# Half of a depthwise convolution's taps on GpSimd, and ten fp32 weight pieces split in two

## The reference

```python
proj = h @ w_in[l]
q, k, v, qi, ki, wi, u, ga, gb = jnp.split(proj, split_at, axis=-1)
y_attn = dsa_attention(q, k, v, qi, ki, wi) @ w_attn_proj[l]     # top 64 keys of a row, softmax over them
y_conv = conformer_conv(u, w_dw[l], b_dw[l], conv_ln_g[l], conv_ln_b[l]) @ w_conv_proj[l]
merged = jax.nn.sigmoid(ga) * y_attn + jax.nn.sigmoid(gb) * y_conv

def conformer_conv(u, w_dw, b_dw, ln_g, ln_b):
    a, g = jnp.split(u, 2, axis=-1)
    z = a * jax.nn.sigmoid(g)
    z = lax.conv_general_dilated(z, w_dw, window_strides=(1,), padding=[(CONV_WIDTH - 1, 0)],
                                 feature_group_count=CONV_CH, ...) + b_dw
    return jax.nn.silu(layernorm(z, ln_g, ln_b))
```

## Time and profile before

| | |
|---|---|
| median of three runs | 954.34 us (953.24 to 954.71) |
| span of the profiled execution, first to last instruction | 953.0 us |
| PE busy | 918.4 us (96%) |
| VectorE busy | 627.9 us (66%) |
| ScalarE busy | 458.5 us (48%) |
| GpSimd busy | 31.7 us (3%), 42 instructions |
| taps on VectorE, L1914 | 120 of 489 ns on average |
| residues on VectorE, L1696 | 267 of 1223 ns |
| native matmuls, L597 | 80 records of 604 ns |
| granted TensorE clock | 0.996 of full speed |

### The profile page before, as it was taken

The page is one execution under the profiler, slowest core; times in us unless marked ns, Lnnn a source line. Parts: engine busy times, 40 slices in busy tenths (PEclk is TensorE's granted clock), DMA queues, the critical chain, the costliest instruction groups (busy, mean ns, idle before and its releaser), DMA issues.

```text
span 953.0 us, 11982 instructions
## 1 busy us (share of the span) xinstructions
PE 918.4 (96%) x4235; PEld 735.6 (77%) x4235; DVE 627.9 (66%) x1022; ACT 458.5 (48%) x709; POOL 31.7 (3%) x42
## 2 busy tenths in 40 slices
PE   4999999999999999999999999999999999999997
PEld 3877755688788888887887777788888788888785
DVE  4898999988755555676748445678656565555444
ACT  0554523465544444443654554674545465555442
POOL 2110000010000000000000000000000000000000
PEclk9999999999999999999999999999999999999999
DMA  9999324656485565575555343455451475655531
GB/s 331 353 386 352 114 79 145 232 204 219 134 265 180 190 192 187 195 263 171 189 190 184 91 152 112 133 177 199 149 204 46 133 221 183 190 193 182 177 133 44
DMA packets 103030, 178.10 MB, mean 187 GB/s; under 512 B 6318, under 2 KB 52635, under 8 KB 102986
## 3 DMA queue, kind: packets, MB, share of 16 engines
q1 hardware_dynamic: 96138, 151.23, 48.2%
q0 software_dynamic: 6848, 26.28, 7.5%
HBM read 176.39 MB, written 1.05 MB: 186 GB/s over the span
## 4 chain that ended last, share of the span: by engine, by line
PE 74%; DVE 12%; issue 7%; DMA 3%; ACT 2%; SPq 0%; POOL 0%; DVEq 0%; POOLq 0%; ACTq 0%
PE bank L564 18%; PE bank L566 18%; PE bank L565 18%; PE bank L976 10%; DVE conv_out L1914 5%; DVE w_lo L1696 2%; DMA tap_rows<-in_w_dw 1%; DMA raw_weights<-in_w_in 1%; ACT w_hi L1232 1%; PE bank L955 1%; DVE ada_acc L1772 1%; PE bank L643 1%; DMA ada_raw<-in_w_ada 1%; PE bank L795 1%; PE bank L635 1%
## 5 line engine op out<-in xcount | busy, mean ns | idle before, releaser
L1696 DVE TENSOR_TENSOR w_lo<-raw_weights,w_hi 128x1024 fp32r<-128x1024 f32 x267 | 324.2, 1223 | 229.2 <-ACT w_hi L1232 227.8
L1232 ACT ACTIVATE w_hi<-raw_weights 128x1024 fp32r<-128x1024 f32 x267 | 281.0, 1059 | 282.1 <-PE bank L566 200.3
L564 PE MATMUL bank<-w_hi,a_hi 128*128 128x512 f32 x808 | 323.5, 400 | 3.1 <-issue 1.3
L566 PE MATMUL bank<-w_hi,a_lo 128*128 128x512 f32 x808 | 315.9, 391 | 0.0
L565 PE MATMUL bank<-w_lo,a_hi 128*128 128x512 f32 x808 | 315.6, 391 | 0.0
L564 PEld LDWEIGHTS bank<-w_hi,a_hi 128*128 128x128 f32 x808 | 152.1, 188 | 40.6 <-issue 8.5
L566 PEld LDWEIGHTS bank<-w_hi,a_lo 128*128 128x128 f32 x808 | 152.1, 188 | 32.7
L565 PEld LDWEIGHTS bank<-w_lo,a_hi 128*128 128x128 f32 x808 | 152.4, 189 | 29.7 <-issue 0.2
L976 PE MATMUL bank<-w_hi,ff_hi 128*128 128x512 f32 x176 | 55.1, 394 | 0.8 <-DVE hidden_rows L2194 0.5
L976 PE MATMUL bank<-w_lo,ff_hi 128*128 128x512 f32 x176 | 54.2, 389 | 0.0
L976 PE MATMUL bank<-w_hi,ff_lo 128*128 128x512 f32 x176 | 54.2, 389 | 0.0
(11 more groups left out here) (264 smaller groups left out, 860.2 us busy)
## 6 DMA issues: line engine op xcount, KB each, us to landing
raw_weights<-in_w_in SPq DMA_DIRECT2D x40, 1024.0 KB, 5.1
raw_weights<-in_w_ffn_in SPq DMA_DIRECT2D x44, 512.0 KB, 4.6
raw_weights<-in_w_gate_up SPq DMA_DIRECT2D x44, 512.0 KB, 4.6
ada_start<-in_w_ada POOLq DMA_DIRECT2D x11, 1024.0 KB, 10.8
raw_weights<-in_w_ffn_out SPq DMA_DIRECT2D x9, 1024.0 KB, 4.9
raw_weights<-in_w_down SPq DMA_DIRECT2D x9, 1024.0 KB, 4.9
ada_raw<-in_w_ada POOLq DMA_DIRECT2D x8, 1024.0 KB, 8.3
raw_weights<-in_w_out SPq DMA_DIRECT2D x8, 1024.0 KB, 5.1
```

The lines of the kernel that those rows point to most:

```text
L564: pe.matmul(ps, hi[:, kt, ts], wh, start=start, stop=False)
L566: return pe.matmul(ps, lo[:, kt, ts], wh, start=False, stop=stop)
L1232: act.activation(w_hi[:, slot, 0:m], raw[:, b % RAW, half * PIECE:half * PIECE + m], ACT.Copy)\
L1696: dve.tensor_tensor(w_lo[:, slot, 0:m], raw[:, b % RAW, half * PIECE:half * PIECE + m], w_hi[:, slot, 0:m], ALU.subtract).then_inc(lo_read ...
```

## The change

Three things go together.

1. **`CG_DVE = 2`.** VectorE does only the taps of groups 0 and 1, 62 in place of 124. `A1_TAPS` becomes 1, eight times 4, and 3, so that they end in step 9; the 26 taps beside the selection stay in number and place.
2. **GpSimd does groups 2 and 3**, in a new `conv_taps` between its blocks 17 and 18. It has no single instruction for multiply and add here, so a tap is a `tensor_scalar` into one of four slots of `tap_products` (128x256) and a `tensor_tensor` that adds the slot to `conv_out`; with two first taps that carry the bias that is 62 and 60 instructions. Each has its own wait: an addition for its product and for the addition before it to the same group, a product for the addition that last used its slot. `tap_products` lies in the memory of `final_g`, so the load of `norm_final_g` moves on SP's queue from among the weights to behind `conv_lo`. `ln_mean` on PE waits for both engines.
3. **`NATIVE_LAST = 24`** leaves no native piece: pieces 25 to 34 are rounded by ScalarE, have residues on VectorE and three products on PE. Block 17 needs no wait for them.

```diff
-NATIVE_FIRST, NATIVE_LAST = 25, 34
+NATIVE_FIRST, NATIVE_LAST = 25, 24
-A1_TAPS = (1,) + (9,) * 10 + (7,)
+A1_TAPS = (1,) + (4,) * 8 + (3,)
...
-    final_g = sb("final_gain_rows", [P, D])
+    final_at = region(D * 4)
+    final_g = sb("final_gain_rows", [P, D], at=final_at)
+    tap_products = sb("tap_products", [P, 4, SEQ], at=final_at)
...
-        sp.dma_start(final_g[:], a["norm_final_g"].partition_broadcast(P)).then_inc(final_landed, 16)
...
         sp.wait_ge(sem["conv_lo"], 2)
+        sp.dma_start(final_g[:], a["norm_final_g"].partition_broadcast(P)).then_inc(final_landed, 16)
         sp.dma_start(mem_rows[:], a["mem_2"].rearrange("o (t p) d -> p (o t) d", p=P)).then_inc(sem["mem_landed"], 16)
...
-            if n == 17:
-                pool.wait_ge(piece_used, NATIVE_LAST + 1)
...
-        for n in range(14, 20):
+        for n in range(14, 18):
+            ada_block(n)
+
+        def conv_taps():
+            pool.wait_ge(sem["pad_zeroed"], 1)
+            pool.wait_ge(sem["conv_in"], 2)
+            pool.wait_ge(sem["vec_copied"], 2)
+            half = CG - CG_DVE
+            total = half * TAPS
+            for g in range(CG_DVE, CG):
+                pool.tensor_scalar(conv_out[:, g, :], conv_in[:, g, 0:SEQ], taps[:, g, 0:1],
+                                   vt[:, V_BDW + g:V_BDW + g + 1], ALU.mult, ALU.add).then_inc(sem["conv_done_pool"], 1)
+            for m in range(half, total + 1):
+                if m < total:
+                    g, k = CG_DVE + m % half, m // half
+                    if m >= half + 4:
+                        pool.wait_ge(sem["conv_done_pool"], m - 3)
+                    pool.tensor_scalar(tap_products[:, m % 4, :], conv_in[:, g, k:k + SEQ], taps[:, g, k:k + 1], None,
+                                       ALU.mult).then_inc(sem["conv_product"], 1)
+                if m > half:
+                    q = m - 1
+                    g = CG_DVE + q % half
+                    pool.wait_ge(sem["conv_product"], q - half + 1)
+                    pool.wait_ge(sem["conv_done_pool"], q - half + 1)
+                    pool.tensor_tensor(conv_out[:, g, :], conv_out[:, g, :], tap_products[:, q % 4, :], ALU.add)                        .then_inc(sem["conv_done_pool"], 1)
+
+        conv_taps()
+        for n in range(18, 20):
             ada_block(n)
...
-            pe.wait_ge(sem["conv_done"], CG * TAPS)
+            pe.wait_ge(sem["conv_done"], CG_DVE * TAPS)
+            pe.wait_ge(sem["conv_done_pool"], (CG - CG_DVE) * TAPS)
...
-            for m in range(taps_done[0], min(taps_done[0] + n, CG * TAPS)):
-                g, k = m % CG, m // CG
+            for m in range(taps_done[0], min(taps_done[0] + n, CG_DVE * TAPS)):
+                g, k = m % CG_DVE, m // CG_DVE
```

More of the change, by code:

```diff
@@ L27 @@
 CG = 4
+CG_DVE = 2
 NEG = -1e38
@@ L1912, in conv_taps @@
                 else:
-                    dve.wait_ge(sem["conv_done"], m - CG + 1)
+                    dve.wait_ge(sem["conv_done"], m - CG_DVE + 1)
                     dve.scalar_tensor_tensor(out=conv_out[:, g, :], in0=conv_in[:, g, k:k + SEQ], scalar=taps[:, g, k:k + 1],
                                              in1=conv_out[:, g, :], op0=ALU.mult, op1=ALU.add).then_inc(sem["conv_done"], 1)
-            taps_done[0] = min(taps_done[0] + n, CG * TAPS)
+            taps_done[0] = min(taps_done[0] + n, CG_DVE * TAPS)
         top_steps = [0]
@@ L2049, in _ @@
                     late_products(3)
-        assert taps_done[0] == CG * TAPS, taps_done
+        assert taps_done[0] == CG_DVE * TAPS, taps_done
         def head_outputs(tag, n_steps, heads, banks_of, dst, done):
```

## The result

The changed kernel takes 994.43 us (median of five runs, 993.09 to 995.45) against 954.71 us in the same comparison (953.24 to 955.35): 1.0411 times as long, 95% interval 1.0395 to 1.0426, or 39.7 us more. The profiled execution spans 992.6 us, 39.6 more than before.

The account below looks back on a forecast made before the run. With PE and VectorE full before, the prediction took SBUF reading shared with GpSimd as the new bound: 101.7 + 70 + 56 = 227.8, plus 6.3 and 4.0, 238.1 against 200.92 us: +37, 991 us, range 955 to 1020.

Parts of the forecast that it names:

- The time of one GpSimd instruction: For GpSimd's 122 tap instructions from 101.7 us on: 0.46 us each, 56 us in all; bounds 0.36 and 0.70 us.
- All of VectorE's 70 us on the road: From 101.7 us to the loop's end, VectorE's taps, residues and other work counted in full against GpSimd's: 70 us.
- the road: SBUF reading shared by VectorE and GpSimd, never both at once; GpSimd through at 227.8 us; 78%.
- p: Time of one of GpSimd's 122 instructions while VectorE is idle; taken as 0.46 us.
- Rival B: No contention, but GpSimd slow by itself: loses time above 0.73 us an instruction; at 0.85 us +15, 969 us; 7%.
- theory 1: The prediction's own: VectorE and GpSimd can't read SBUF at the same time, so each costs the other time.
- the main case: VectorE and GpSimd share one road to SBUF, which bounds the loop: +37 us, 991 us; 78%.
- Rival A: The engines share after all: long GpSimd instructions run beside VectorE, through at 158 us; -3.6 us, 950.7 us; 15%.
- Rival C: Shared road with a short hold, 0.30 to 0.36 us an instruction: +18 to +25, 972 to 979 us; no own chance.
- Without GpSimd's part: Selection and loop, split pieces and fewer VectorE taps: 3.9 - 5.4 - 2.1 = -3.6 us, `y_rows` turned at 197.3.
- Beside the selection: Four residues of 1.14 us move VectorE's first maximum by 4.6 us to 136.4; first turn at 137.4, 3.9 us lost.
- Block 18: After GpSimd's taps: 6.3 us of issue and transfer, then 4.0 us from its use to the turn of `y_rows`.

Follow-up runs that it names:

- no_dve_taps: The changed kernel without VectorE's 60 accumulating taps, GpSimd's 122 instructions all kept: 991.96 us, ratio 1.0391 to the kernel before.
- no_pool: The changed kernel without GpSimd's 122 tap instructions, groups 2 and 3 of the convolution a constant: 953.6 us, ratio 0.9981 to the kernel before.
- one_group_work: The changed kernel with GpSimd doing the taps of group 2 only, 61 instructions, group 3 a constant: 965.23 us, ratio 1.0102 to the kernel before.
- write_late: The changed kernel with GpSimd's 122 instructions only writing constants, started after VectorE's two first taps: 970.46 us, ratio 1.0151 to the kernel before.
- write_only: The changed kernel with each of GpSimd's 122 instructions replaced by writing a 128x256 constant, reading nothing: 983.81 us, ratio 1.0297 to the kernel before.

## Why the prediction was right, and where it was not

The time (994.4 against 991) and the place of the loss are as predicted: `y_rows` turned at 238.92 against 238.1. But that the time came so close is luck: two terms of the sum were wrong, by 41 us and by 39 the other way, and made up for each other. Right was the mechanism, that the two engines wait for each other's reads, and what follows it, block 18 and the turn of `y_rows`.

*The time of one GpSimd instruction* was the larger error. The step took 0.46 us from a power of one number, with 0.36 to 0.70 as bounds; unhindered it is 0.795, outside the bounds. That is 122 x 0.335 = 41 us too little. The addition, 0.70 us apart, was at my upper end. The product failed: the lower bound had it on a level with VectorE's, 0.31 us, and it takes 0.89, longer than the addition with its two inputs. The Trainium skill (GPSIMD Engine Reference, "Performance versus the Vector engine") gave an estimate of 0.78 us for the addition, nearer than mine.

*All of VectorE's 70 us on the road* was the error the other way. Hindrance came to 30.8 us, not 70: 39 us too much. The assumption was that an instruction of either engine occupies the road for all of its length. The trace denies it. When VectorE's last reading ahead of the wait ended, at 207.5 us, GpSimd had done 94 instructions: 74.7 us at its own pace, which with VectorE's 70 would fill 145 us of road. They took 105.8 (101.58 to 207.39), so 39 us passed side by side. One part of that is the product, which lets VectorE through before it ends (the tap at 106.81, the residue at 109.00). Another is the start of an instruction: the tap at 107.49 began beside the addition and needed only 0.29 us more when that was over. How the 39 us divide between the two was not measured. From 207.5 us on VectorE stood idle and the road was empty. With p = 0.795 the prediction's sum would have been 41 us higher, 1032 us. `no_dve_taps` points the same way: 24 us of VectorE's reads less gave GpSimd 7 at most.

*Rival B*, slow by itself: its condition (p over 0.73 us) was met, and its price at 0.795 is 101.6 + 97.0 + 10.3 - 200.9 = 8 us. The other 30 are contention, so the main case stands, but B's 7% were too few: its condition and theory 1 were not exclusive. *Rival A* falls: VectorE is stretched. *Rival C* put the hold below the instruction's length, which is right of products and not of additions, yet set p with it, which is not right.

*Without GpSimd's part*: -3.6 us predicted at the turn of `y_rows`, -1.7 measured (`no_pool`). The first maximum was good (135.89 against 136.4), so was the first turn (136.77 against 137.4). The loop from first turn to mean took 60.5 us against 65.4 before, 4.9 less and not 7.5: the step left out that PE, after waiting 4.2 us for that first turn, runs at the lower clock. Its small work up to the next piece took 3.41 us (136.77 to 140.18; 1.74 before), 0.46 of them another wait, and that piece 1.5 us too long.

*Beside the selection* I counted contention only in GpSimd's favour or not at all: the first maximum was kept at 136.4, though "whoever waits for whom" puts VectorE's waits there. After the change it is at 144.28, 8.4 us behind `no_pool`, and PE idles 11.21 us ("5 or more" was announced). In this kernel that cost is hidden behind GpSimd's own end; in `one_group_work` it is the whole loss, about 10 us.

*Block 18*: 6.3 + 4.0 us predicted from GpSimd's last addition to PE's turn; measured 238.92 - 229.39 = 9.5. Right.

So the 38.0 us are, in order: -1.7 for the rest of the change (the mean over the channels at 197.25 in `no_pool` against 198.94), +12.4 for what GpSimd does to the selection and the loop (PE was through with it at 209.61, which is 229.70 less 20.09 of idle time), +20.1 until GpSimd is through (229.70), and +7.2 for block 18 and two steps of PE at the lower clock (9.2 us from there to the turn, against 2.0). The last three are where PE stood, not what each cause alone would give back: without the 12.4, GpSimd would still be through at 229 us, or little earlier. The other 1.6 us of the span lie behind that turn and were not traced. The moved load of `norm_final_g` is in `no_pool` too, which is no slower for it.

## What to carry to other kernels

Before work goes to GpSimd, two numbers are needed, and they differ: its own time for an instruction (here 0.70 and 0.89 us for 128x256), which decides when it is through, and how long it holds the reads that it shares with VectorE (here to the end of an addition, and only the first part of a product), which decides what VectorE loses. A neighbour with other operations on 128x1 or 128x2 gives neither. VectorE's work here was mostly instructions with two SBUF inputs, and moving half of the taps to GpSimd left it nearly as busy as it was. So first ask what the free case would win: here 0.2%. No run tried an instruction of GpSimd that multiplies and adds two tensors at once, so the two numbers are for a tap in two instructions.

## What the runs showed of the hardware that was not expected

- On GpSimd a multiplication of 128x256 fp32 by a number per partition takes 0.92 us (0.89 apart), an addition of two such tiles 0.72 (0.70 apart), and writing a constant 0.32 (0.25 apart). Yet the additions disturb VectorE more: 0.16 against 0.06 us each up to the first maximum.
- After the change a tap or residue of VectorE that an addition of GpSimd held up ended 0.28 or 1.08 us behind the addition's end, in all 35 cases to within 0.01 us. One that began 0.43 us or more behind a product's start was not held by it.
- Before the changed part begins, the twelve traces already differ by up to 2.5 us (GpSimd requests block 16 at 90.7 to 93.2 us). So a difference of 2 us between two single traces says nothing unless it is taken from such a mark.
- A TENSOR_SCALAR of VectorE from SBUF to SBUF beside a gapless stream of constants on GpSimd stood 16.35 us in `write_late` and 29.14 us in `write_only`, until the stream ended; beside GpSimd's reading instructions the same first taps were not held up like that.
- After 4.2 us of idle time PE's matmuls with 512 columns were 0.42 us apart in place of 0.24, up to 6.5 us behind the wait's end (`no_pool`). In the changed kernel the granted clock is 0.77 from 131 to 145 us and 0.59 from 220 to 240 us, around waits of 11.2 and 20.1 us.
